# Expert values of a PEER layer: 26 of 64 pairs of weight blocks by seven block products

## The reference, cut to what matters

```
idx = top 16 experts of each head;  g = softmax(top scores)
act = gelu(h . expert_u[idx])
out = sum over the picked experts of (g * act) * expert_v[idx]      # (256, 1024)
result = rms_norm(x + out) * norm_final
```

## Time and profile before

| | |
|---|---|
| median of 3 runs | 1962.53 us (1961.2 to 1962.88) |
| the profiled execution, its own time | 1965.11 us |
| its span, first to last instruction | 1963.3 us |
| PE busy | 1901.9 us (97%) |
| DVE busy | 1397.2 us (71%) |
| ACT busy | 1145.7 us (58%) |
| POOL busy | 403.0 us (21%) |
| mean granted TensorE clock | 0.991 |
| mean DMA rate | 181 GB/s |

### The profile page before, as it was taken

How to read it: one execution, slowest core, us unless ns; L and a number is a source line. 1 busy time by engine, 2 the same in 40 slices (tenths; PEclk the granted TensorE clock), 3 DMA queues, 4 the chain that set the end, 5 groups by cost and what they waited for, 6 DMA issues and landing times. The chain is left out here.

```text
span 1963.3 us, 34673 instructions
## 1 busy us (share of the span) xinstructions
PE 1901.9 (97%) x14088; PEld 1771.1 (90%) x14088; DVE 1397.2 (71%) x2526; ACT 1145.7 (58%) x1943; POOL 403.0 (21%) x395
## 2 busy tenths in 40 slices
PE   8999999899999789999999999999999999999997
PEld 5798999898888789999899999999999998888886
DVE  6787776877777687557856578999987755555554
ACT  4865544556777455445755554477777754444544
POOL 0010011002332200012101200068859920000000
PEclk9999999999999899999999999999999999999999
DMA  9465787346453557666444455554454455555553
GB/s 362 169 203 184 253 279 263 127 151 191 154 168 121 184 172 232 187 187 230 140 151 151 149 164 179 187 162 151 151 162 140 143 167 186 191 185 191 188 187 118
DMA packets 97742, 356.23 MB, mean 181 GB/s; under 512 B 11104, under 2 KB 11232, under 8 KB 97200
## 3 DMA queue, kind: packets, MB, share of 16 engines
q1 hardware_dynamic: 84240, 305.04, 47.4%
q0 software_dynamic: 12624, 48.08, 7.7%
q10 hardware_dynamic: 720, 0.91, 0.1%
HBM read 352.94 MB, written 1.05 MB: 180 GB/s over the span
## 5 line engine op out<-in xcount | busy, mean ns | idle before, releaser
L2180 DVE TENSOR_TENSOR wl<-raw,wh 128x1024 fp32r<-128x1024 f32 (+1 forms) x566 | 693.8, 1230 | 369.4 <-ACT wh L1475 368.0
L1475 ACT ACTIVATE wh<-raw 128x1024 fp32r<-128x1024 f32 (+1 forms) x566 | 593.6, 1050 | 413.4 <-PE psum L602 368.3
L600 PE MATMUL psum<-peer_hh,wh 128*128 128x256 f32 x1024 | 295.6, 289 | 0.0
L602 PE MATMUL psum<-peer_hh,wl 128*128 128x256 f32 x1024 | 290.4, 284 | 0.0
L601 PE MATMUL psum<-peer_hl,wh 128*128 128x256 f32 x1024 | 290.4, 284 | 0.0
L601 PE MATMUL psum<-wl,csh 128*128 128x512 f32 x512 | 202.0, 394 | 0.0
L600 PE MATMUL psum<-wh,csh 128*128 128x512 f32 x512 | 201.8, 394 | 0.0
L602 PE MATMUL psum<-wh,csl 128*128 128x512 f32 x512 | 201.8, 394 | 0.0
L600 PEld LDWEIGHTS psum<-peer_hh,wh 128*128 128x128 f32 x1024 | 194.4, 190 | 0.0
L601 PEld LDWEIGHTS psum<-peer_hl,wh 128*128 128x128 f32 x1024 | 194.3, 190 | 0.0
L602 PEld LDWEIGHTS psum<-peer_hh,wl 128*128 128x128 f32 x1024 | 194.2, 190 | 0.0
(11 more groups left out here) (478 smaller groups left out, 4823.6 us busy)
## 6 DMA issues: line engine op xcount, KB each, us to landing
raw<-in_mlp_w SPq DMA_DIRECT2D x128, 512.0 KB, 4.2
raw<-in_eu SPq DMA_DIRECT2D x128, 512.0 KB, 3.4
raw<-in_ev SPq DMA_DIRECT2D x128, 512.0 KB, 3.3
araw<-in_ada_w POOLq DMA_DIRECT2D x76, 512.0 KB, 4.5
raw<-in_dil_qk SPq DMA_DIRECT2D x48, 512.0 KB, 4.2
raw<-in_dil_v SPq DMA_DIRECT2D x24, 512.0 KB, 3.5
raw<-in_w_in SPq DMA_DIRECT2D x16, 512.0 KB, 3.4
raw<-in_w_query SPq DMA_DIRECT2D x16, 512.0 KB, 3.5
```

The costliest lines, as they stand in the source:

```text
L600: e.matmul(o, l[0], r[0], start=start, stop=False, skip_group_check=loose)
L602: i = e.matmul(o, l[1], r[0], start=False, stop=stop, skip_group_check=loose)
L1475: e.activation(b.wh[v % NSPLIT][:, 0:cols], b.raw[v % NRAW][:, 0:cols], ACT.Copy).then_inc(S.hi, 1)
L2180: e.tensor_tensor(b.wl[v % NSPLIT][:, 0:cols], b.raw[v % NRAW][:, 0:cols], b.wh[v % NSPLIT][:, 0:cols].bitcast(F32), ALU.subtract).then_in ...
```

## The change

**Seven products for a pair.** For 26 pairs of groups (i, i+1), i = 16, 20, ..., 116, the product of the 2 x 2 blocks (token halves by the two groups of C; the two groups by column halves of V) is formed by seven block products in place of eight, after Strassen and Winograd. It needs four sums S1 to S4 of coefficient blocks (128 x 128 each) and four sums T1 to T4 of half weight blocks (128 x 512 each), which GpSimd forms from `C3` and from `raw`, the T sums into the unused `xT`. Four more PSUM banks (`seven`) gather the products that several quarters of the output share; they are added to the output by VectorE near the end (`U`). The order of the steps is now a list `EV` of 180 entries: `n` is a group as before (12 matmuls), and a pair is `b11` (3 matmuls, half a unit to split), `b2` (6), `t12` (6) and `t34` (6). All seven-product pairs stand between two pairs of the old kind. T sums are split like a unit (`t12` and `t34`), S sums like a coefficient block of 512 columns (`S hi`, `S lo`).

**More buffers and other waits.** From entry 14 on there are five pairs of split buffers instead of three, and six `cs` pairs instead of four; a coefficient block is split just ahead of its own unit. SP waits, before it reuses a `raw` buffer of a seven-product pair, for GpSimd's last read of it.

**The two small changes.** The last three groups run first for all of the first token half and then for the second, and each half of the output is normed by itself, from an SBUF copy `xt`. In `dil_order()` one tick is moved from ahead of the tail to its entry 5 (another there only gets another name), and the second half of the last `scores` and `probs` moves back by one entry.

The diff, cut to its core:

```diff
-        if z in (0, 2) or z == 4 and c in (0, 8):
+        if z in (0, 2) or z == 4 and c == 0 or z in (4, 5) and c == 8:
             out.append(("tick", c, z))
...
-    out += [("tick", 8, 6), ("tick", 8, 7)]
-    tail = [[("pv", 6, 0), ("pv", 6, 1), ("scores", 7, 0), ("scores", 7, 1), ("out", 6, 0)],
-            [("probs", 7, 0), ("probs", 7, 1)], [("turn", 7, 0)], [("turn", 7, 1), ("pv", 7, 0)],
-            [("pv", 7, 1), ("out", 7, 0)], [], [], []]
+    tail = [[("pv", 6, 0), ("pv", 6, 1), ("scores", 7, 0), ("out", 6, 0)], [("scores", 7, 1), ("probs", 7, 0)],
+            [("probs", 7, 1), ("turn", 7, 0)], [("turn", 7, 1), ("pv", 7, 0)], [("pv", 7, 1), ("out", 7, 0)], [], [], []]
     for i, steps in enumerate(tail):
         out += steps + [("dil_w_o", i, 0)]
-        out += [("tick", 9, i)] * (0, 1, 2, 2, 2, 1, 0, 0)[i]
+        out += [("tick", 9, i)] * (0, 1, 2, 2, 2, 2, 0, 0)[i]
...
+SEVEN = range(16, 118, 4)
...
+def ev_order():
+
+    out = [("n", i) for i in range(16)]
+    for i in SEVEN:
+        out += [("b11", i), ("b2", i + 1), ("t12", i), ("t34", i), ("n", i + 2), ("n", i + 3)]
+    return out + [("n", i) for i in range(120, 128)]
+
+
+EV = ev_order()
+EV_AT = {key: v for v, key in enumerate(EV)}
+EV_FIVE = 14
+EV_RING = [(EV0 + EV_FIVE + z) % NSPLIT for z in range(NSPLIT)] + [3, 4]
+EV_SLOT = [(EV0 + v) % NSPLIT if v < EV_FIVE else EV_RING[(v - EV_FIVE) % 5] for v in range(len(EV))]
+EV_PREV = [max([w for w in range(v) if EV_SLOT[w] == EV_SLOT[v]], default=None) for v in range(len(EV))]
...
-    m.cs = near + far
+            fourth = pair("slot", UNIT, tt)
+    m.cs = near[0:2] + far + near[2:4]
+    m.slots = [[h, l] for h, l in zip(b.wh, b.wl)]
+    m.slots += [fourth, fifth]
...
+        def sums(i, z):
+            pe.wait_ge(S.dve, at["S lo", i])
+            return sp(m.Sp, z, 128)
+
+        def product(o, x, w, first=False, last=False):
+            e.matmul(o, x[0], w[0], start=first, stop=False, skip_group_check=True)
+            e.matmul(o, x[0], w[1], start=False, stop=False, skip_group_check=True)
+            return e.matmul(o, x[1], w[0], start=False, stop=last, skip_group_check=True)
+
+        for v, (kind, i) in enumerate(EV[:-NSPLIT]):
+            pe.wait_ge(S.lo, EV0 + v + 1)
+            left, right = [sp(m.slots[EV_SLOT[v]], 0, 1024, z, 512) for z in (0, 512)]
+            first, last = i == SEVEN[0], i == SEVEN[-1]
+            if kind == "n":
+                for t in range(2):
+                    x = coefficients(i, t)
+                    product(acc[t][0], x, left)
+                    done = product(acc[t][1], x, right)
+            elif kind == "b11":
+                if first:
+                    seven = {z: take("seven", z) for z in (1, 5, 6, 7)}
+                done = product(seven[1], coefficients(i, 0), left, first, last)
+            elif kind == "b2":
+                product(acc[0][0], coefficients(i, 0), left)
+                done = product(acc[0][1], sums(i - 1, 3), right)
+            elif kind == "t12":
+                product(seven[5], sums(i, 0), left, first, last)
+                done = product(seven[6], sums(i, 1), right, first, last)
+            else:
+                product(seven[7], sums(i, 2), left, first, last)
+                done = product(acc[1][0], coefficients(i + 1, 1), right)
+            done.then_inc(S.unit, 1)
+        for t in range(2):
+            for v in range(len(EV) - NSPLIT, len(EV)):
+                i = EV[v][1]
+                pe.wait_ge(S.lo, EV0 + v + 1)
+                x = coefficients(i, t)
                 for h in range(2):
-                    mm3(acc[t][h], sp(m.cs[i % 4], 0, 256, t * 128, 128), wsp(j, h * 512, 512), False, i == 127,
-                        unit=t == 1 and h == 1, loose=True)
+                    done = product(acc[t][h], x, sp(m.slots[EV_SLOT[v]], 0, 1024, h * 512, 512), False, i == 127)
+                if t == 1:
+                    done.then_inc(S.unit, 1)
+                elif i == 127:
+                    done.then_inc(S.pe, 1)
+                    n[0] += 1
+                    at["ev", "first tokens"] = n[0]
...
+        for v, (kind, i) in enumerate(EV):
+            if kind not in ("t12", "t34"):
+                coef_high(i)
+            if kind == "b2":
+                ac.wait_ge(S.pool, at["S", i - 1])
+                if i - 1 > SEVEN[0]:
+                    ac.wait_ge(S.unit, EV0 + EV_AT["t34", i - 5] + 1)
+                act(m.Sp[0], m.S, ACT.Copy, mark=("S hi", i - 1))
+            if v >= AHEAD:
+                ev_high(v, kind, i)
+            if (kind, i) == ("n", 123):
+                ac.wait_ge(S.unit, EV0 + EV_AT["t34", SEVEN[-1]] + 1)
+                act(m.U[0], bank("seven", 1), ACT.Copy, mark=("seven", 1))
...
+                ac.wait_ge(S.dve, at["final add", t, h])
+                act(m.fsq, m.xt[:, t, h * 512:h * 512 + 512], ACT.Square, scale=1.0 / 32,
+                    accum_out=m.fs[:, 2 * t + h:2 * t + h + 1], mark=("final square", t))
+            ac.wait_ge(S.dve, at["final sum", t])
+            act(m.gs[:, t:t + 1], m.fs[:, 4 + t:5 + t], ACT.Sqrt, bias=eps, mark=("final sqrt", t))
+
+    def ev_high(v, kind, i):
...
+            ac.wait_ge(S.unit, EV0 + min(0, v - NSPLIT + 1))
+            if EV_SLOT[v] == 4:
+                ac.wait_ge(S.dve, at["coef", 7])
+        else:
+            ac.wait_ge(S.unit, EV0 + EV_PREV[v] + 1)
+        high, low = ev_pair(b, v, 512 if kind == "b11" else 1024)
+        e.activation(high, src, ACT.Copy).then_inc(S.hi, 1)
...
+            ac.wait_ge(S.unit, EV0 + (ev_last(i - 6) + 1 if i >= 6 else 0))
+        act(m.cs[i % 6][0], m.C3[:, i, :], ACT.Copy, mark=("coef hi", i))
...
+            tt(m.cs[i % 6][1], m.C3[:, i, :], m.cs[i % 6][0].bitcast(F32), ALU.subtract, mark=("coef", i))
+
+        for v, (kind, i) in enumerate(EV):
+            if kind not in ("t12", "t34"):
+                coef_low(i)
+            if kind == "b2":
+                ve.wait_ge(S.act, at["S hi", i - 1])
+                tt(m.Sp[1], m.S, m.Sp[0].bitcast(F32), ALU.subtract, mark=("S lo", i - 1))
+            if v >= AHEAD:
+                high, low = ev_pair(b, v, 512 if kind == "b11" else 1024)
+                ve.wait_ge(S.hi, EV0 + v + 1)
+                e.tensor_tensor(low, ev_source(b, kind, i), high.bitcast(F32), ALU.subtract).then_inc(S.lo, 1)
+            if (kind, i) == ("n", 123):
+                ve.wait_ge(S.act, at["seven", 1])
+                tt(m.U[1], bank("seven", 6), m.U[0], ALU.add)
+                own()
+                tt(m.U[2], bank("seven", 7), m.U[1], ALU.add)
+                tt(m.U[3], bank("seven", 5), m.U[1], ALU.add)
+                own()
+                tt(m.U[4], bank("seven", 5), m.U[2], ALU.add)
...
+            if t:
+                ve.wait_ge(S.unit, EV0 + len(EV))
+            else:
+                ve.wait_ge(S.pe, at["ev", "first tokens"])
+            own()
+            for h in range(2):
+                tt(m.xt[:, t, h * 512:h * 512 + 512], bank("acc", t, h), m.U[((0, 3), (2, 4))[t][h]], ALU.add,
+                   mark=("final add", t, h))
+            ve.wait_ge(S.act, at["final square", t])
+            tt(m.fs[:, 4 + t:5 + t], m.fs[:, 2 * t:2 * t + 1], m.fs[:, 2 * t + 1:2 * t + 2], ALU.add,
+               mark=("final sum", t))
+            ve.wait_ge(S.act, at["final sqrt", t])
+            recip(m.gs[:, 2 + t:3 + t], m.gs[:, t:t + 1])
+            own()
             for h in range(2):
                 z = slice(h * 512, h * 512 + 512)
-                stt(xt[:, t, z], bank("acc", t, h), m.gs[:, 2 + t:3 + t], m.nf[:, z], ALU.mult, ALU.mult,
+                stt(m.xt[:, t, z], m.xt[:, t, z], m.gs[:, 2 + t:3 + t], m.nf[:, z], ALU.mult, ALU.mult,
...
+        for i in SEVEN:
+            A11, A21, A12, A22 = [m.C3[:, i + z, t:t + 128] for z in range(2) for t in (0, 128)]
+            if i == SEVEN[0]:
+                po.wait_ge(S.dve, at["coef", 13])
+            else:
+                po.wait_ge(S.dve, at["S lo", i - 4])
+            tt(S1, A21, A22, ALU.add, ("S", i))
+            tt(S3, A11, A21, ALU.subtract, ("S", i))
+            own()
+            tt(S2, S1, A11, ALU.subtract, ("S", i))
+            own()
+            tt(S4, A12, S2, ALU.subtract, ("S", i))
+            ra, rb = [b.raw[(EV0 + i + z) % NRAW] for z in range(2)]
+            for z in range(2):
+                u = EV0 + i + z
+                po.wait_ge(S.raw[u % NRAW], 16 * (u // NRAW + 1))
+                if z == 0:
+                    if i > SEVEN[0]:
+                        po.wait_ge(S.lo, EV0 + EV_AT["t34", i - 4] + 1)
+                    tt(T1, ra[:, 512:1024], ra[:, 0:512], ALU.subtract, ("T", "first", i))
+            tt(T3, rb[:, 512:1024], ra[:, 512:1024], ALU.subtract, ("T", "left", i))
+            own()
+            tt(T2, rb[:, 512:1024], T1, ALU.subtract, ("T", "t12", i))
+            own()
+            tt(T4, rb[:, 0:512], T2, ALU.subtract, ("T", "t34", i))
...
+        i = u - NRAW - EV0
```

(54 more changed lines are left out.)

24 lines of the change are left out of this document (5 added, 19 removed).

## The result

| | before | after |
|---|---|---|
| median of the runs, us | 1962.41 (1961.20 to 1962.88) | 2015.88 (2015.79 to 2017.22) |
| profiled execution, its own time / span, us | 1965.11 / 1963.3 | 2015.83 / 2014.0 |
| granted clock, mean | 0.991 | 0.995 |

The ratio is 1.027 (95% interval 1.0255 to 1.0285). The change makes the kernel 2.7% slower, 53.5 us by the medians; 49.5 us were forecast, a time of 2012 us.

A forecast was written before the change was run, and what follows sets the result against it. TensorE bound the kernel; after the change VectorE, slowed by turns with GpSimd, would bound the value stage. +58 us there, -7 at the dilated mixer's end and -1.5 at the kernel's end gave +49.5 on 1962.5: 2012 us, range 1958 to 2055.

The forecast's parts named there:

- VectorE becomes the bound, through turns: Value stage: GpSimd's reads make VectorE wait, 5.4 us a period; VectorE sets a period of 13.6 us, above TensorE's 10.46.
- The price of a turn: Value stage: each GpSimd operation costs VectorE time, 1.05 us for 512 columns and 0.29 for 128.
- The stage: Value stage: 25 periods of 13.6 us plus its ends give 342.9 us against 284.6, so 58 us longer.
- Late T sums cost nothing: Value stage: GpSimd's T sums come in time, with 1.8 us to spare before T12 is needed, so costed at nothing.
- The dilated end: End of the dilated mixer: of 13.9 us of TensorE's waits about 8 remain; gain 7 us, bounds 3 and 10.
- The step on the clock: End of the dilated mixer: 1 us less for the half clock (0.50 from 665.20) that follows the long wait.
- The end: After the last matmul: norming by halves takes 5.6 us where it was 7.4; gain 1.5 us, bounds 1.8 and -0.8.
- (a): Rival, value stage: VectorE and GpSimd hardly hinder each other, TensorE stays the bound, 1936 us; chance 0.13.
- (b): Rival, value stage: VectorE and GpSimd exclude each other for whole durations, period 16.2 us, 2077 us; chance 0.03.
- (c): Rival, value stage: waits of about 1 us bring TensorE's clock to the lower level, +240 us, about 2195; chance 0.01.
- (d): Rival, value stage: turns cost about 3.4 us a period, the small changes' gain is lost, 1962 us; chance 0.04.
- break-even of 11.6: Value stage: a period of 11.6 us, turns costing 3.4, at which the whole change neither gains nor loses.

The follow-up runs named there:

- t_written: Changed kernel with GpSimd's four T operations per pair turned into zero fills that read nothing, T sums left out: 1933.93 us, 0.9846 of the kernel before.
- t_half: Changed kernel with two of the four T operations per pair cut to one column, all waits kept: 1959.42 us, 0.9989 of the kernel before.
- ve_sums: Changed kernel with VectorE forming all S and T sums itself and GpSimd idle in the stage: 1968.98 us, 1.0024 of the kernel before.
- ve_sums6: Changed kernel with one pair in six groups (17 pairs) and all sums on VectorE: 1949.97 us, 0.9939 of the kernel before.
- ve_sums5: Changed kernel with one pair in five groups (21 pairs) and all sums on VectorE: 1953.67 us, 0.9953 of the kernel before.
- t_one_input: Changed kernel with each T operation replaced by a scaled copy of one block, T sums left out: 1951.48 us, 0.9938 of the kernel before.
- three small runs: The kernel before with only the new dilated order, only the tick moved, or new order plus split end: 1956.81, 1961.72 and 1954.64 us.

## Why the prediction was right

The mechanism held, and the sizes of the value stage were within a tenth; those of the two small changes were further off. The total is closer than its terms: the stage cost 3.3 us more than forecast and the dilated end gave 1.9 more back, and 2.8 us of the 53.5 lie in no stretch of the two traces but between medians and profiled executions.

- **VectorE becomes the bound, through turns.** Right: busy for 364.47 of 365 us; period 13.68 us for 13.6. Shown by t_written (no reads, no cost) and t_half (half of the operations, half of the cost), and not only by the fit of the sum.
- **The price of a turn.** 512 columns cost 1.10 us, for 1.05 taken from the excess in the earlier trace rows; 128 columns 0.27 for 0.29. The 0.29 was the one price without a row of its shape, drawn from a line through the two others. With the 0.54 for 256 columns this is about 2.15 ns a column and nearly nothing fixed. The price is not in any row of the groups by line; it came from distances between starts on one engine while the other was working. What GpSimd's 512 columns would last was forecast less well: 1.87 us for about 2.1. VectorE's splits of 1024 last 1.21 to 2.32 us, 1.67 to 1.70 in the mean, for 1.6 to 2.2.
- **The stage.** +61.3 us for +58. 25 x 0.08 = 2.0 us is the period; the remaining 1.3 lies at the stage's ends.
- **Late T sums cost nothing.** Right. ScalarE's waits for GpSimd (34.2 and 19.5 us in 200) appeared, yet VectorE had no idle time.
- **The dilated end.** -8.9 us for -7, inside 3 to 10. The waits left are 3.9 + 1.4 + 0.3 = 5.6 us where I had about 8; below they stand as the profile after gives them:

```profile
PE psum L655 <- POOL work L3318: 3.9, 4, 1.3
PE psum L641 <- DVE col L2266: 1.4, 1, 1.4
PE psum L641 <- DVE dil_o L2266: 0.3, 1, 0.3
```

I had kept most of the `col` wait of 3.6 us, and 1.4 of it was left. The step on the clock was wrong: 1 us of the gain was for a half clock that would go with the long wait. It stayed. In the profile after, TensorE waits 1.22 and 0.89 us for GpSimd's products before 662.20 and 663.74, and from 664.1 to about 667.6 the granted clock is at its lower level again (0.50 in the windows of 665 to 667 us), some 3.5 us where it was 4.2.

- **The end.** -1.3 us for -1.5. ScalarE loads its table once, as assumed.
- **The rivals.** (a) would be 1936 us: t_written, without the turns, is at 1933.93. (b), whole durations, would need 1.29 us and, by estimate, 0.45 us a turn and falls with 1.10 and 0.27. The Trainium skill's rule that the two exclude each other for the whole instruction ("SBUF — State Buffer", section "Who interferes with whom") has the right direction here, and is too much by 0.19 us for an operation of 512 columns. (c) fell: the clock in the window above is 1.00, though TensorE waits up to 1.1 us and its weight loads up to 1.5. (d) fell, as the turns cost 5.5 us a period and not 3.4; t_half and ve_sums, at periods of 11.49 and 11.68 us beside the break-even of 11.6, show that such a cost does give a time like that of before.

Some expectations behind the prediction missed. I sized ve_sums6 and ve_sums5 by work alone and overlooked that a wait for a landing in VectorE's queue stands ahead of its splits; the prediction had looked at such waits in SP's queue. One input cost less than half of two in t_one_input. The three small runs missed their ranges by 1 to 3 us; in their traces the untouched stretch behind the second MLP is longer, for a reason that stays open.

## What to carry to other kernels

Before giving work to an engine that idles, ask what it reads: a two-input GpSimd operation of 512 columns took 1.10 us from a VectorE that would have done the same in 0.60. Where the helper or VectorE itself must take more than the bound engine leaves over, thin the change out: 13 pairs won 0.8%, 17 won 0.4% with the sums on GpSimd and 1.0% with late sums on VectorE, and 26 lost 2.7%. The two small changes alone won 0.5% of that, so the 0.4% shows no gain by the products. And place what waits for a landing as late in an in-order queue as its result allows: the same sums moved behind one split took TensorE's loss in the stage from 5.6 us to 0.8.

## What the runs showed that I had not expected

- One input is much cheaper than half: 0.41 us for 512 columns, against 1.10 with two. GpSimd's own time is not: the one-input `TENSOR_SCALAR` needs 1.88 us there, as long as the two-input operations of the changed kernel (1.87).
- A GpSimd fill of 1.81 us beside VectorE, at 96% busy, slows it by nothing that shows.
- In the value stage 88 waits of the weight loads in 200 us, up to 1.5 us each, and 44 of the matmuls, up to 1.1 us, left the granted clock at 1.00 over 365 us, with TensorE busy for 85%. In the dilated mixer's end of the same profile two waits of 1.22 and 0.89 us, with 0.98 of 2 us busy between 660 and 662, came just before a fall to 0.50. What tells the two apart was not tried.
